# Gated-delta scan: two per-direction chains over PSUM bank pairs, and a new order for the pieces between them

## The reference, cut to what matters

```
tmat = strict_lower(kb kc^T * decay) + I          # per chunk and head
w = solve(tmat, kb * exp(gc)) ; u = solve(tmat, vc * beta)
# scan over the chunks, in order:
v_new = u - w s
o     = qg s + qk v_new
s     = s * exp(g_last) + kd^T v_new
```

## Time and profile before

| | us |
|---|---|
| median of 3 runs | 1946.89 |
| the three runs | 1947.01, 1946.89, 1941.97 |
| the profiled execution, device time | 1942.07 |
| its span, first to last instruction | 1939.9 |

### The profile page before, as it was taken

One profiled execution on the slowest core, in us unless ns is written; L12 is line 12 of the kernel. 1 busy time (PEld: TensorE's weight loads), 2 busy tenths in 40 slices (PEclk: granted clock), 3 DMA queues, 4 the chain that ended last, 5 costly groups with the idle time before them and its releaser, 6 DMA issues.

```text
span 1939.9 us, 41539 instructions
## 1 busy us (share of the span) xinstructions
PE 1833.6 (95%) x17621; PEld 1150.2 (59%) x17621; DVE 729.0 (38%) x1523; ACT 500.7 (26%) x1133; POOL 376.8 (19%) x506
## 2 busy tenths in 40 slices
PE   6999999999999998999999999999888899999998
PEld 4565556677787554565556445556577764455454
DVE  3145333444553335111121425334465632522323
ACT  3212532343332223001111231353433221200010
POOL 1612000244452001310011032200254610100000
PEclk7999999999999999999999999999899999999999
DMA  9410000164555316889998412000300022499996
GB/s 323 142 57 22 22 1 1 47 212 154 181 172 163 136 44 233 307 330 366 359 364 312 148 44 66 22 0 1 99 14 25 13 89 74 173 411 411 410 411 253
DMA packets 139545, 320.67 MB, mean 165 GB/s; under 512 B 10760, under 2 KB 97582, under 8 KB 124046
## 3 DMA queue, kind: packets, MB, share of 16 engines
q1 hardware_dynamic: 127584, 287.20, 40.0%
q0 software_dynamic: 6432, 20.00, 3.7%
q10 hardware_dynamic: 5390, 11.44, 1.7%
HBM read 305.45 MB, written 13.16 MB: 164 GB/s over the span
## 4 chain that ended last, share of the span: by engine, by line
PE 84%; DVE 6%; issue 4%; ACT 3%; DMA 2%; SPq 1%; POOL 0%; ACTq 0%; DVEq 0%; POOLq 0%
PE psum L610 17%; PE psum L1143 11%; PE psum L1045 7%; PE psum L1174 6%; PE psum L730 3%; PE psum L1152 3%; PE psum L914 3%; PE psum L1224 3%; PE psum L547 2%; PE psum L751 2%; PE psum L896 2%; PE psum L1186 2%; PE psum L807 1%; PE psum L531 1%; PE psum L831 1%
## 5 line engine op out<-in xcount | busy, mean ns | idle before, releaser
L610 PE MATMUL psum<-hT,ring 128*128 128x256 f32 (+2 forms) x976 | 337.7, 503 | 4.3 <-ACT hT L1518 3.8
L610 PEld LDWEIGHTS psum<-hT,ring 128*128 128x128 f32 (+1 forms) x976 | 184.4, 191 | 145.3 <-issue 127.6
L1143 PE MATMUL psum<-ring,arena 128*64 128x256 f32 x1536 | 174.9, 384 | 5.8 <-issue 2.0
L1143 PEld LDWEIGHTS psum<-ring,arena 128*64 128x64 f32 x1536 | 111.1, 138 | 66.6 <-issue 17.4
L1045 PE MATMUL psum<-hT,ring 128*128 128x512 f32 (+1 forms) x384 | 139.4, 521 | 0.9 <-DVE xT L2323 0.9
L2410 DVE TENSOR_TENSOR arena<-arena,psum 128x384 f32<-128x384 f32 (+1 forms) x32 | 15.6, 488 | 260.7 <-PE psum L1152 161.6
L1045 PEld LDWEIGHTS psum<-hT,ring 128*128 128x128 f32 x384 | 72.7, 190 | 64.8 <-issue 61.5
L914 PE MATMUL psum<-wbuf,ring 64*64 64x64 f32 x1920 | 78.4, 229 | 31.3 <-DVE wbuf L2288 25.6
L1795 ACT COPY ring<-psum 128x256 f32<-128x256 f32 x240 | 73.4, 383 | 97.4 <-PE psum L914 97.4
L914 PEld LDWEIGHTS psum<-wbuf,ring 64*64 64x64 f32 x1920 | 68.9, 141 | 37.9 <-issue 35.8
L2717 POOL DMA_INDIRECT big<-h_rows_lat,idx x16 | 15.7, 979 | 381.7 <-PE psum L1248 173.7
(11 more groups left out here) (351 smaller groups left out, 3386.7 us busy)
## 6 DMA issues: line engine op xcount, KB each, us to landing
ring<-in_moe_w_gate SPq DMA_DIRECT2D x64, 1024.0 KB, 10.9
ring<-in_ada_w SPq DMA_DIRECT2D x48, 1024.0 KB, 5.4
ring<-in_moe_w_up SPq DMA_DIRECT2D x32, 1024.0 KB, 9.1
hT<-in_moe_w_down SPq DMA_DIRECT2D x24, 1024.0 KB, 12.2
ring<-in_w_in SPq DMA_DIRECT2D x20, 1024.0 KB, 6.5
big<-in_moe_w_up SPq DMA_DIRECT2D x16, 1024.0 KB
sz<-in_moe_w_down SPq DMA_DIRECT2D x16, 1024.0 KB
big<-in_moe_w_down SPq DMA_DIRECT2D x16, 1024.0 KB, 14.4
```

The source lines that it names most:

```text
L610: m = pe.matmul(b[0:c1 - c0, 0:n], lhsT=w[:, k, c0:c1], rhs=hT[:, k, t0:t0 + n], start=k == 0, stop=k == KD - 1)
L1143: m = pe.matmul(b[e * CAP_L:(e + 1) * CAP_L, 0:2 * P], lhsT=xs[:, k, e, 0:CAP_L], rhs=w[e][:, 2 * (k - ks[0]) + q, :], start=k == 0, stop= ...
```

## The change

Products: `zo` and `zd` become one product per direction, `("z", l, j, n, d)`, over two neighbouring banks; `x` and `xb` of a direction become one product over two banks. The factor of a direction waits only for the update of that direction, and the update only for the subtraction of its direction. VectorE subtracts per direction, and ScalarE copies with one instruction of 128x512 where it had two of 128x256. VectorE's pieces of slot 2n-2 and 2n-1 follow the subtraction of level n. `kv` is split into `kr` and `vr`, and the table is dealt out anew. The scaling of the state moves to GpSimd (`decay_state`), and VectorE adds with one instruction. The decay rows are fetched in slots 2 and 3.

```diff
 BETWEEN = (
-    (("wt", 0), ("wt", 1)), (("v", 0), ("v", 1)), (("go", 0),), (("go", 1),), (("st", 0), ("st", 1)),
-    (("g", 0),), (("g", 1),), (), (("kk", 0),), (("kv", 0),), (("kk", 1), ("qk", 0)), (("qk", 1),), (("kv", 1),))
+    (("wt", 0), ("wt", 1)), (("v", 0), ("v", 1)), (("go", 0),), (("go", 1),), (("st", 0),),
+    (("st", 1), ("g", 0)), (("g", 1), ("kr", 0)), (("vr", 0),), (("kk", 0),), (("kk", 1),), (("kr", 1),), (("qk", 0),),
+    (("qk", 1), ("vr", 1)))
...
# TensorE
+                def level_factor(j, n, x, d):
+                    key = ("z", l, j, n, d)
+                    bs = claim_two(key).rearrange("p (a c) -> p a c", a=2)
+                    if n > 1:
+                        evacuated(pe, ("x", l, j, d, n - 1))
...
                 def level_update(j, n, x, d):
-                    keys = ("x", l, j, d, n), ("xb", l, j, d, n)
-                    bs = [claim(key) for key in keys]
-                    for kind in range(2):
-                        evacuated(pe, ("zd" if kind else "zo", l, j, n))
+                    key = ("x", l, j, d, n)
+                    bs = claim_two(key).rearrange("p (a c) -> p a c", a=2)
+                    evacuated(pe, ("z", l, j, n, d))
...
-                        level_factor(j, n, x)
+                        for d in range(2):
+                            level_factor(j, n, x, d)
...
# ScalarE
-                    if slot == 4 and 1 <= j < NT - 1:
-                        for d in range(2):
-                            decay_rows(j + 1, d)
+                    if slot in (2, 3) and 1 <= j < NT - 1:
+                        decay_rows(j + 1, slot - 2)
...
-                            for w, name in ((GH, "xb"), (0, "x")):
-                                key = (name, l, j, d, n)
-                                b = product_ready(act, key)[:, 0:GH * HALF]
+                            key = ("x", l, j, d, n)
+                            b = two_banks(act, key)[:, :, 0:GH * HALF]
...
# VectorE
-                            for h in range(GH):
-                                m = dve.scalar_tensor_tensor(out=S[:, d, h, :], in0=S[:, d, h, :],
-                                                             scalar=gt4[:, j % 2, d, 1, h:h + 1],
-                                                             in1=b[:, h * P:(h + 1) * P], op0=ALU.mult, op1=ALU.add)
-                            read_out(m, key)
+                            dve.wait_ge(s["sdec"], 2 * (j - 1) + d + 1)
+                            x = S[:, d, :, :].rearrange("p h c -> p (h c)")
+                            read_out(dve.tensor_tensor(x, x, b, ALU.add), key)
...
-                    gdn_between(j, 0)
                     for n in range(1, LEVELS - 1):
-                        for h0, name in ((0, "zo"), (2, "zd")):
...
+                        for d in range(2):
+                            key = ("z", l, j, n, d)
...
+                        gdn_between(j, 2 * n - 2)
                         gdn_between(j, 2 * n - 1)
-                        gdn_between(j, 2 * n)
+                    gdn_between(j, 2 * LEVELS - 4)
                     gdn_between(j, 2 * LEVELS - 3)
...
# GpSimd
+                def decay_state(j):
+                    for d in range(2):
+                        if need_ctx or tile_of(d, j) >= CT:
+                            product_ready(pool, ("go", l, j, d))
+                        else:
+                            product_ready(pool, ("v", l, j, d))
+                        x = S[:, d, :, :]
+                        pool.tensor_tensor(x, x, gt4[:, j % 2, d, 1, :].unsqueeze(2).to_broadcast([P, GH, P]), ALU.mult
+                                           ).then_inc(s["sdec"], 1)
...
                         masked(n, j)
+                        if n == 3 and j >= 2:
+                            decay_state(j - 1)
```

More of the change, by code:

```diff
@@ L338, in build_program @@
                  "lmul", "egc", "xg", "dex", "eb", "dm", "x0", "xd", "away", "ml", "qg", "osq", "mixd", "rmax",
-                 "rexp", "aff", "top", "hrow", "att", "tok", "idx", "gath", "grow", "gr0", "gr1", "cur", "scat", "arow", "S", "dve", "pool_e"]
+                 "rexp", "aff", "top", "hrow", "att", "tok", "idx", "gath", "sdec", "grow", "gr0", "gr1", "cur", "scat", "arow", "S", "dve", "pool_e"]
         FIRST_ALONE = ("zero", "zrow", "scat", "arow")
@@ L389, in scores_ready, with two_banks @@
             return psum[:, b:b + 2, :].rearrange("p a c -> p (a c)")[:, 0:(CT if i < CT else NT) * P]
+        def two_banks(eng, key):
+            product_ready(eng, key)
+            b = where[key][0]
+            return psum[:, b:b + 2, :]
         def attended(eng, l, calls, n):
@@ L407, in between @@
             for what, d in BETWEEN[slot]:
-                i = j + {"wt": -1, "v": -1, "go": -1, "st": -1, "kv": 0}.get(what, 1)
+                i = j + {"wt": -1, "v": -1, "go": -1, "st": -1, "kr": 0, "vr": 0}.get(what, 1)
                 if 0 <= i < NT:
@@ L811, in gdn_piece @@
                             o, lhsT=qkvT[:, GH + h, t], rhs=qkvT[:, h, t], start=True, stop=True))
-                    elif what == "kv":
+                    elif what == "kr":
                         if j == 0 and d == 0:
@@ L815, in gdn_piece @@
                         heads(("kr", l, j, d), lambda o, h: pe.transpose(o, qkvT[:, GH + h, t], ident[:, :]))
+                    elif what == "vr":
                         heads(("vr", l, j, d), lambda o, h: pe.transpose(o, qkvT[:, 2 * GH + h, t], ident[:, :]))
@@ new lines, in level_factor @@
+                def level_factor(j, n, x, d):
[3 more added lines that the diff above has]
+                        evacuated(pe, ("x", l, j, d, n - 1))
+                    elif d == 0:
+                        evacuated(pe, ("t0o", l, j))
+                        evacuated(pe, ("t0d", l, j))
+                    for pair in ((0, 3), (1, 2)):
+                        for kind, h in enumerate(pair):
+                            c = h % 2 * HALF
+                            for k in range(2):
+                                t, o = rows_of[k ^ xt_half(h, n)], rows_of[k ^ x_half(h, n)]
+                                m = pe.matmul(bs[o, kind, c:c + HALF], lhsT=gML[n % 2][t, d, h, :],
+                                              rhs=x[t, d, XTB[h], :], start=True, stop=True)
+                    done(m, key)
@@ L2177, in gdn_piece @@
                         read_out(dve.tensor_tensor(x, b, x, ALU.mult), key)
-                    elif what == "kv":
-                        key = ("kr", l, j, d)
+                    elif what == "kr":
                         b = product_ready(dve, key).rearrange("p (h c) -> p h c", h=GH)
@@ L2184, in gdn_piece @@
                             [P, GH, P]), ALU.mult), key)
-                        key = ("vr", l, j, d)
+                    elif what == "vr":
                         b = product_ready(dve, key).rearrange("p (h c) -> p h c", h=GH)
```

38 lines of the change are left out of this document (7 added, 31 removed).

## The result

| | median us (runs) | ratio to before, 95% interval |
|---|---|---|
| before | 1943.62 (20) | |
| after | 1952.69 (20) | 1.0047 (1.0037 to 1.0058) |

The account below looks back on a forecast made before the run. TensorE, busy 1833.6 of 1939.9 us, was taken as the bound, with a chain of waits partly binding the second scan. Terms -13.2 + 1.4 = -11.8, taken as -12, gave 1946.9 - 12 = 1935 us; range 1924 to 1949.

Parts of the forecast that it names:

- Rival 2: First layer: bank waits of 2 us each for `kr0` and `kk0` make the kernel 7 us slower, 1954; chance 0.15.
- The prediction's own sign of being wrong: First scan: iterations growing by over 1 us would refute the forecast, one of three such signs.
- First layer, +1.4 forecast: First scan: four iterations, each 0.35 us longer through bank waits, cost 1.4 us.
- the list of bank waits: First layer: updates of levels 3, 4, 5 take banks of `st0`, `kr0`, `kk0`; factor of level 5 that of `vr0`.
- The walk: Step-by-step timing of one iteration: first layer 0.35 us longer, second layer 2.0 or 1.2 us shorter.
- The `kr0` term: First layer, level 4: the update waits for `kr0`'s bank from 6.5 to 7.55 us.
- The `kk0` wait: Level 5: the update waits for `kk0`'s bank, 13.0 to 13.9 us in the first layer, 9.0 to 10.45 in the second.
- a rival on the good side only: Second layer, iteration 0: 2.4 GHz kept or regained early gives about 5 us on top, 1929; chance 0.10.
- about as long: Second scan: the stretch at the lower clock was to keep about its length.
- Second layer, -13.2 forecast: Second scan: iterations 0 to 5 save 3.0, 2.4, 2.2, 1.8, 1.8 and 2.0 us, 13.2 in all.
- the 5 to 12 foretold: Second scan: waits for VectorE's reads of `kk`, `vr` and `kr`, 5 to 12 us, replace waits for the subtraction.
- GpSimd's scaling at nothing: Both layers: two added GpSimd instructions in four iterations each, 1.28 us apiece, stay covered and cost nothing.

Follow-up runs that it names:

- The first: Changed kernel with the conditioning half ahead of the piece in the first layer's odd slots, read out before the decay DMA in slot 3: ratio 0.9974.
- the control: Kernel before the change, with only the conditioning half moved ahead of the piece in odd slots of the first layer: ratio 0.9973, 1938.99 against 1943.52 us.
- the best version: Kernel before, plus the two chains over bank pairs and the conditioning half ahead of the piece in odd slots: ratio 0.9923, 1925.32 against 1939.53 us.

## Why the prediction was wrong

It forecast 1935, faster by 12 us; the kernel got slower by 9 us. Rival 2, that the first layer pays for banks, comes nearest, and its second-layer gain of 6 was 5.5. But that its 7 us slower lies near the 9 measured is partly luck. It took waits of 2 us each for `kr0` and `kk0`, where 1.78 and 0.59 were measured. The rest came from a bank and a clock that it does not name. The prediction's own sign of being wrong, first-layer iterations longer by over 1 us, came true in iterations 2 to 4, by 3.7 to 4.7 us.

- **First layer, +1.4 forecast, +14.7 in the profiles.** The step that failed is the list of bank waits. I counted the banks and named four pieces (`kr0`, `kk0`, `st0`, `vr0`), but not the conditioning product, whose bank stands in the same pairs and is left only at the end of each odd slot, right ahead of the update. It is no piece of the table, and I took its read-out as done. The runs showed a wait of 0.57 us for it at levels 1 and 3. The first and the control experiment give it about 9 us (5 to 13), clock included.
- **What an iteration's 4.3 us are made of.** Iteration 3: waits of 0.57, 0.57, 1.78 and 0.59 us, 3.5 in all, less the 1.0 of before, and 1.7 for a stretch of 3.4 us at half clock: 4.2. The walk had two waits of 1.0 and 0.9 in place of one of 1.0 and called the sum 0.35 longer, so it also counted on about 0.6 gained elsewhere in the chain. That gain did not show in this full stretch.
- **The `kr0` term** was walked as 1.0 us and was 1.78. `g1` was priced at 0.75, with the slot it had before. In its new place, behind the subtraction of level 4, it meets GpSimd's decay and takes 1.6. I had weighed the shared ports only for the new scaling, not for old instructions that meet in a new order. The row of 0.91 us against 0.68 was the warning. Moving `kr0` ahead regained 6.8 us in the first scan, clock included.
- **The `kk0` wait** was walked as 0.9 (0.59 measured, shared with the conditioning bank) in the first scan and 1.45 in the second (9.0 to 10.45; 1.03 to 1.08 measured).
- **The clock** had a rival on the good side only. With the new idle, 3.6 us in an iteration that had 1.0, a stretch of 3.4 us at half the clock stands in each of iterations 2 to 4 of the first scan, at 1.7 us each, and in iterations 1 and 3 of the second. No term held that. What was expected of iteration 0 of the second scan was wrong on the other side: its stretch at the lower clock, called "about as long", fell from 17.1 to 10.2 us. Over each whole scan the clock moved little: from 13.6 to 17.0 us at half clock in the first, from 20.5 to 17.0 in the second. Half the difference is an estimate of its net price: 1.7 us lost in the first scan and as much gained in the second.
- **Second layer, -13.2 forecast, -5.5 measured.** The mechanism was right: waits for the subtraction went from 24.4 to 0.6 us, and iterations 2 and 4, with the clock at 1.00, took 28.9 and 31.8 us where the walk gave 28.9 and 31.6. Iterations 1 and 3, with a dip of the clock each, took 30.0 and 34.2 instead of 26.1 and 31.6. Iteration 1 waited 1.35 us for `kr0` and 1.75 ahead of the update of level 5, iteration 3 waited 1.41 for `vr0` behind the slow `g1`. Iteration 0 gained 0.9, not 3; it waited 2.2 us for `kr0`. The waits for `kk`, `kr` and `vr` came to 9.2 us, inside the 5 to 12 foretold.
- **GpSimd's scaling at nothing** holds: giving it back changed nothing measurable. What was underrated is the meeting of two older instructions. The Trainium skill (SBUF — State Buffer, "Who interferes with whom") calls the port pair that VectorE and GpSimd share an exclusive lock. The trace agrees: L2158 and GpSimd's decay end at 532.16 and 532.13 us. The cost was 0.85 us, not 0.2.
- **The parts.** Chains alone: ratio 1.0000, with +12.6 and -9.1 us in the two scans. All the rest of the change with single banks: 0.9995. Together, 1.0047, they were worse than each.

## What to carry to other kernels

When products take more PSUM banks from one ring, list for every claim who held each bank last and when that holder is read, including holders that are not in the table one is editing; what ends just ahead of a claim on an in-order engine is the one that stalls. Give such a holder's read-out something to hide behind: a few lines of order turned a neutral change into 14 us less, of which the order alone, by the control, is some 5. Cost the full stretch and the waiting stretch apart: the same chains cost 12.6 us in the first scan and gained 9.1 in the second.

## What the runs showed of the hardware

- A VectorE instruction on four columns with two SBUF operands (L2158) took 1.00 us instead of 0.15 beside a GpSimd instruction of 128x512, itself 1.46 instead of 1.04, and the two ended within 0.03 us of each other. The GpSimd instruction had begun beside the VectorE instruction ahead of it (L2155, 530.55 to 531.24, two SBUF operands as well), and its usual 1.04 us fit in behind that one. With `kr0` moved between them, L2158 took 0.15 and GpSimd 1.04.
- In iterations with idle of 0.57, 0.57 and 1.78 us, a stretch of 3.4 us at half the clock followed: `kk0` took 2.07 us in place of 1.16. With one wait of 1.88 ahead of `kk0` and none of 0.57, it took 1.16. In the best version's stretch above, without idle, the clock stayed at 1.00.
- One ScalarE copy of 128x512 from two PSUM banks takes 588 ns on average, where one of 128x256 takes 386. The saving is smaller than 772 less 588, since copies in a row overlap in the trace: four of 128x256 took 1.20 us from first start to last end, two of 128x512 took 1.07 to 1.08.
